# One hybrid attention/recurrence layer stack on one core: the compression of the samples' cached rows by three products of split operands in place of one full-precision product

## The reference, cut to what matters

```python
kc = compress(full(0), lp["cmp_pe"][0], lp["cmp_w1"][0], lp["cmp_w2"][0])
vc = compress(full(1), lp["cmp_pe"][1], lp["cmp_w1"][1], lp["cmp_w2"][1])
```

## Time and profile before

| | |
|---|---|
| median of 3 runs | 2860.48 us (2852.64 to 2863.11) |
| the profiled execution | 2857.92 us, its span 2855.9 us |
| mean granted TensorE clock | 0.861 of full |
| first layer: paired stage | 274 to 925 us; its compression steps lie between 274 and 557 us |
| second layer: the same | from 1694 us; its compression steps lie between 1694 and 1978 us |
| busy share | PE 81%, DVE 43%, ACT 28%, POOL 5% |

### The profile page before, as it was taken

How to read it: one execution, slowest core, us unless ns; L and a number is a source line. 1 busy time by engine, 2 the same in 40 slices (tenths; PEclk the granted TensorE clock), 3 DMA queues, 4 the chain that set the end, 5 groups by cost and what they waited for, 6 DMA issues and landing times.

```text
span 2855.9 us, 55193 instructions
## 1 busy us (share of the span) xinstructions
PE 2309.5 (81%) x22254; PEld 2086.2 (73%) x22254; DVE 1217.4 (43%) x1985; ACT 788.4 (28%) x1386; POOL 156.3 (5%) x233
## 2 busy tenths in 40 slices
PE   6986897867566889999679868878575677999995
PEld 6985676755455889999679857767453556999995
DVE  3233426254455354452332244252645454544523
ACT  3212323232223232242132132232323233322321
POOL 1000000000010000000010000000000100000000
PEclk9986898968678999999889868988686789999998
DMA  3362221212221122223123712212222211223232
GB/s 113 97 163 78 60 60 60 60 51 67 63 60 40 62 67 97 89 84 102 48 77 96 193 42 60 66 54 60 60 64 57 67 40 55 81 90 93 85 97 70
DMA packets 172775, 216.45 MB, mean 76 GB/s; under 512 B 39009, under 2 KB 138594, under 8 KB 171106
## 3 DMA queue, kind: packets, MB, share of 16 engines
q1 hardware_dynamic: 172514, 212.87, 24.9%
HBM read 204.57 MB, written 16.59 MB: 77 GB/s over the span
## 4 chain that ended last, share of the span: by engine, by line
PE 71%; DVE 16%; ACT 6%; SPq 3%; issue 3%; DMA 1%; DVEq 0%; ACTq 0%
PE ps L657 13%; PE ps L659 13%; PE ps L658 13%; PE ps L926 7%; PE ps L901 2%; PE ps L674 2%; SPq L539 2%; PE ps L819 2%; PE ps L828 1%; PE ps L894 1%; DVE arena L1631 1%; PE ps L721 1%; DVE arena L1428 1%; DVE rstd L1370 1%; DVE hf_lo L1399 1%
## 5 line engine op out<-in xcount | busy, mean ns | idle before, releaser
L657 PE MATMUL ps<-hm_hi,ring_hi 128*128 128x260 f32 x2432 | 695.5, 286 | 54.7 <-DVE hm_lo L1399 54.7
L659 PE MATMUL ps<-hm_hi,ring_lo 128*128 128x260 f32 x2432 | 692.6, 285 | 0.0
L658 PE MATMUL ps<-hm_lo,ring_hi 128*128 128x260 f32 x2432 | 690.6, 284 | 0.0
L1392 DVE TENSOR_TENSOR ring_lo<-ring,ring_hi 128x1024 fp32r<-128x1024 f32 x200 | 244.8, 1225 | 726.6 <-ACT ring_hi L1075 725.9
L657 PEld LDWEIGHTS ps<-hm_hi,ring_hi 128*128 128x128 f32 x2432 | 463.9, 191 | 57.3 <-issue 57.0
L658 PEld LDWEIGHTS ps<-hm_lo,ring_hi 128*128 128x128 f32 x2432 | 463.5, 191 | 0.3
L659 PEld LDWEIGHTS ps<-hm_hi,ring_lo 128*128 128x128 f32 x2432 | 463.4, 191 | 0.0
L1075 ACT ACTIVATE ring_hi<-ring 128x1024 fp32r<-128x1024 f32 x200 | 211.5, 1059 | 685.4 <-PE ps L659 681.6
L657 PE MATMUL ps<-hf_hi,ring_hi 128*128 128x260 f32 x704 | 203.2, 289 | 8.4 <-DVE hf_lo L1399 8.2
L659 PE MATMUL ps<-hf_hi,ring_lo 128*128 128x260 f32 x704 | 200.6, 285 | 0.0
L658 PE MATMUL ps<-hf_lo,ring_hi 128*128 128x260 f32 x704 | 200.4, 285 | 0.0
(11 more groups left out here) (362 smaller groups left out, 3943.6 us busy)
## 6 DMA issues: line engine op xcount, KB each, us to landing
ring<-in_w SPq DMA_DIRECT2D x202, 512.0 KB, 3.6
arena<-in_kv_cmp SPq DMA_DIRECT2D x96, 128.0 KB, 2.1
extra<-in_kv_cmp SPq DMA_DIRECT2D x80, 128.0 KB, 2.2
slot<-in_kv_cmp SPq DMA_DIRECT2D x80, 128.0 KB, 2.1
out_win_old<-in_win SPq DMA_DIRECT2D x16, 511.0 KB, 9.8
slot<-in_k_sel SPq DMA_DIRECT2D x96, 64.0 KB, 1.9
arena<-in_k_sel SPq DMA_DIRECT2D x96, 64.0 KB, 1.9
extra<-in_v_sel SPq DMA_DIRECT2D x96, 64.0 KB, 1.8
```

Of the source, the lines that this page charges most:

```text
L657: mmul(out, wh, hi[:, k, cols], start=(k == 0), stop=False)
L658: mmul(out, wh, lo[:, k, cols], start=False, stop=False)
L659: last = mmul(out, wl, hi[:, k, cols], start=False, stop=(ci == len(chunks) - 1 and k == k1 - 1))
L1392: v.tensor_tensor(ring_lo[:, n % RING, :], r, ring_hi[:, n % RING_HI, :], SUB).then_inc(S["w_lo"], 1)
```

## The change

Both operands of the chunk steps are split into an fp32r part and an fp32r remainder, and each of the eight fp32 matmuls becomes three fp32r matmuls (24 in a step, still 128 weight columns by 128 moving columns). The weights are split once in each layer (two steps `w1_split`: three ScalarE copies, three VectorE subtractions of 1024, 512 and 512 columns), each chunk's rows once (32 steps `chunk_split` in a layer: one ScalarE copy and one VectorE subtraction of 128x1024). The copy goes to one half of `ring_hi`, so the third slot is not used by the compression; the remainder goes over the rows in the slot. Chunk `n + 2` is split right after chunk `n` in the list, and its copy waits until chunk `n` has been read (`cmp_h`). In the planner a chunk step now weighs 2 and a split 1, where a chunk step weighed 4. The host lays out the pages so that the 16 columns of one product stand side by side. Units 0 and 1 alone are loaded ahead; unit `u` of the compression waits for the read of unit `u - 2`. The weights' copy goes over a part of `nsa` and waits for its store (`kv_stored`).

```diff
-    st = [(("qz", 0), 1)]
+    st = [(("w1_split", 0), 1), (("w1_split", 1), 1), (("qz", 0), 1), (("chunk_split", 0), 1), (("chunk_split", 1), 1)]
     for b in range(DEC):
-        st += [(("chunks", (b, q)), 4) for q in range(4)]
+        for q in range(4):
+            st += [(("chunks", (b, q)), 2)]
+            if 4 * b + q + 2 < 4 * DEC:
+                st += [(("chunk_split", 4 * b + q + 2), 1)]
+SLOT_OF = [u % 2 if u < U_WK else (u - U_WK) % USLOT for u in range(N_UNIT)]
+def before_in_slot(u):
+    mine = [w for w in range(u) if SLOT_OF[w] == SLOT_OF[u]]
+    return mine[-1] if mine else (U_WK - 1 if SLOT_OF[u] == 2 else None)
+        def units_read(eng, n):
+            if n <= U_WK:
+                eng.wait_ge(S["cmp_h"], 2 * n)
+            else:
+                eng.wait_ge(S["u_used"], n - U_WK)
-            if u >= USLOT:
-                eng.wait_ge(S["u_used"], u - USLOT + 1)
+            if before_in_slot(u) is not None:
+                units_read(eng, before_in_slot(u) + 1)
...
# TensorE, chunks
                         for k in range(STRIDE // 2):
-                            last = mmul(out, w1s[:, c, k, :], slot[:, :, c, :, k::STRIDE // 2], start=(k == 0), stop=(k == STRIDE // 2 - 1))
-                        if c:
-                            last.then_inc(S["u_used"], 1)
+                            mmul(out, w1_hi(c, k), hi[:, :, k, :], start=(k == 0), stop=False)
+                            mmul(out, w1_hi(c, k), lo[:, :, k, :], start=False, stop=False)
+                            last = mmul(out, w1s_lo[:, c, k * P:(k + 1) * P], hi[:, :, k, :], start=False, stop=(k == STRIDE // 2 - 1))
+                        last.then_inc(S["cmp_h"], 1)
...
# ScalarE
+                    if step == "w1_split":
+                        if n == 0:
+                            act.wait_ge(S["w1s_ready"], 32)
+                            act.wait_ge(S["kv_stored"], 16)
+                            A(w1h0[:], smp[:, 0:1024], ACT.Copy).then_inc(S["w1s_hi"], 1)
+                        else:
+                            for h in range(2):
+                                A(w1h1[h][:], smp[:, 1024 + 512 * h:1536 + 512 * h], ACT.Copy).then_inc(S["w1s_hi"], 1)
+                    elif step == "chunk_split":
+                        u, c = divmod(n, 2)
+                        slot = unit_landed(act, u)
+                        if u:
+                            act.wait_ge(S["cmp_h"], n - 1)
+                        A(ring_hi[:, c, :].rearrange("p (n x) -> p n x", n=PAGES // 2), chunk_view(slot, c), ACT.Copy).then_inc(S["chunk_hi"], 1)
...
# VectorE
+                    elif step == "chunk_split":
+                        u, c = divmod(n, 2)
+                        dve.wait_ge(S["chunk_hi"], n + 1)
+                        v.tensor_tensor(chunk_view(slots_lo[u % 2], c), chunk_view(slots[u % 2], c),
+                                        ring_hi[:, c, :].rearrange("p (n x) -> p n x", n=PAGES // 2), SUB).then_inc(S["chunk_lo"], 1)
...
# host
-        "kv_cmp": cache[:, :, 0:2].reshape(DEPTH * N_POOL, PAGE // 2, 2, 2, GROUPS, HD).transpose(0, 2, 5, 3, 4, 1).reshape(DEPTH * N_POOL, P, 2 * PAGE),
+        "kv_cmp": cache[:, :, 0:2].reshape(DEPTH * N_POOL, 8, STRIDE // 2, 2, 2, GROUPS, HD).transpose(0, 3, 6, 4, 2, 5, 1).reshape(DEPTH * N_POOL, P, 2 * PAGE),
```

More of the change, by code:

```diff
@@ L278, in build @@
         hm = sb("hm", [P, KB, TOK])
+        nsa_base = nc.sbuf_base
         nsa = sb("nsa", [P, NT, TOK])
@@ L302, in build @@
         arena = sb("arena", [P, ARENA])
+        extra_base = -(-nc.sbuf_base // 32) * 32
         extra = sb("extra", [P, EXTRA])
@@ L398, in build @@
         cm = at(3, HEADS)
+        where[0] += -(arena_base // 4 + where[0]) % 8
+        slot0 = where[0]
         slots = [at(2048), more(2048),
                  nc.alloc_sbuf_tensor_at("slot2", [P, 2048], F32, offset=ring_base + 4 * RING * KB * P)[:]]
+        slots_lo = [at_bytes("slot0_lo", arena_base, slot0, [P, 2048])[:], at_bytes("slot1_lo", extra_base, 0, [P, 2048])[:]]
         kcs = at(DEC, NCS)
@@ L421, in build @@
         w1s = smp[:, 0:2048].rearrange("p (c k e) -> p c k e", c=2, k=STRIDE // 2)
+        w1s_lo = at_bytes("w1s_lo", ring_base, 0, [P, 2, 1024])
+        w1h0 = at_bytes("w1h0", nsa_base, 4 * TOK, [P, 1024])
+        w1h1 = [at_bytes("w1h1", nsa_base, 7 * TOK, [P, 512]), at_bytes("w1h2", nsa_base, 9 * TOK, [P, 512])]
         w2s = smp[:, 2048:2304].rearrange("p (c e) -> p c e", c=2)
@@ L453, in build @@
                  "pc_ok pcp_ok sc_mm mx ex sc_v pt_mm pt_ev pv o_ev qpad_ok ss_mm ss_v ss_a c_free "
-                 "cmp_h cmp_act cmp_o cmp_k mixed ffn_c ffn_act ffn_h ffn_t w_hi w_lo s_hi s_lo trig_ok rs_stored phase_ok dif_ok cmp_b cmp_sum staged_a staged_v w1s_ready u_used kw_new smp_done").split()
+                 "cmp_h cmp_act cmp_o cmp_k mixed ffn_c ffn_act ffn_h ffn_t w_hi w_lo s_hi s_lo trig_ok rs_stored phase_ok dif_ok cmp_b cmp_sum staged_a staged_v w1s_ready w1s_hi w1s_lo kv_stored chunk_hi chunk_lo u_used kw_new smp_done").split()
         S = {n: ctx.enter_context(nc.semaphore(n)) for n in names}
@@ L515, in unit_landed, with w1_hi, chunk_view @@
         def unit_landed(eng, u):
-            eng.wait_ge(c_ready[u % USLOT], 16 * sum(UNIT_DMAS[u % USLOT:u + 1:USLOT]))
-            return slots[u % USLOT]
+            eng.wait_ge(c_ready[SLOT_OF[u]], 16 * sum(n for w, n in enumerate(UNIT_DMAS[:u + 1]) if SLOT_OF[w] == SLOT_OF[u]))
+            return slots[SLOT_OF[u]]
+        def units_read(eng, n):
[3 more added lines that the diff above has]
+                eng.wait_ge(S["u_used"], n - U_WK)
+        def w1_hi(c, k):
+            if c == 0:
+                return w1h0[:, k * P:(k + 1) * P]
+            return w1h1[k // 4][:, k % 4 * P:(k % 4 + 1) * P]
+        def chunk_view(a, c):
+            return a.rearrange("p (n c x) -> p n c x", n=PAGES // 2, c=2)[:, :, c, :]
         def load_unit(eng, kind, l, u):
-            slot, done = slots[u % USLOT], c_ready[u % USLOT]
-            if u >= USLOT:
-                eng.wait_ge(S["u_used"], u - USLOT + 1)
+            slot, done = slots[SLOT_OF[u]], c_ready[SLOT_OF[u]]
+            if before_in_slot(u) is not None:
+                units_read(eng, before_in_slot(u) + 1)
             if U_WK <= u < U_SK:
@@ L587, in _ @@
                 sp.dma_start(smp[:, 2048:2304], I["w2_pairs"][l]).then_inc(S["w1s_ready"], 16)
-                for u in range(USLOT):
+                for u in range(2):
                     load_unit(sp, mybir.EngineType.SP, l, u)
                 sp.wait_ge(S["nsa_ready"], 1)
-                sp.dma_start(O["kv"][l].rearrange("p (a b) -> p a b", a=6), nsa[:, 4:NT, :]).then_inc(S["stores"], 16)
+                sp.dma_start(O["kv"][l].rearrange("p (a b) -> p a b", a=6), nsa[:, 4:NT, :]).then_inc(S["kv_stored"], 16)
                 for b in range(DEC):
@@ L602, in _ @@
                         sp.dma_start(gate_r[r, h, :], gates[QD * h:QD * (h + 1), NQ, :].rearrange("b (h n) -> b h n", n=3)).then_inc(S["gs_ready"], 16)
-                for u in range(USLOT, N_UNIT):
+                for u in range(2, N_UNIT):
                     load_unit(sp, mybir.EngineType.SP, l, u)
@@ L621, in _ @@
                 sp.dma_start(O["conv_s"][l].rearrange("p (a b c) -> p a b c", a=FT, b=2), couts).then_inc(S["stores"], 16)
-                sp.wait_ge(S["stores"], 16 * (4 + DEC))
+                sp.wait_ge(S["stores"], 16 * (3 + DEC))
+                sp.wait_ge(S["kv_stored"], 16)
                 host_meet(S["arrive"], list(S.values()) + list(T.values()) + w_ready + c_ready)
@@ L918, in sample @@
                         b, (half, c) = n[0], divmod(n[1], 2)
-                        if n == (0, 0):
-                            pe.wait_ge(S["w1s_ready"], 32)
-                        elif n[1] == 0:
+                        if half == 0:
+                            pe.wait_ge(S["w1s_lo"], c + 1)
+                        if b and n[1] == 0:
                             pe.wait_ge(S["cmp_k"], b)
-                        slot = unit_landed(pe, 2 * b + half).rearrange("p (n c g t) -> p n c g t", n=PAGES // 2, c=2, g=GROUPS)
+                        u = 2 * b + half
+                        pe.wait_ge(S["chunk_lo"], 2 * u + c + 1)
+                        view = lambda a: a.rearrange("p n (k x) -> p n k x", k=STRIDE // 2)
+                        hi = view(ring_hi[:, c, :].rearrange("p (n x) -> p n x", n=PAGES // 2))
+                        lo = view(chunk_view(slots_lo[u % 2], c))
                         out = W4[:, c, :, CH * half:CH * (half + 1)].rearrange("p g (n t) -> p n g t", n=PAGES // 2)
                         for k in range(STRIDE // 2):
-                            last = mmul(out, w1s[:, c, k, :], slot[:, :, c, :, k::STRIDE // 2], start=(k == 0), stop=(k == STRIDE // 2 - 1))
-                        if c:
-                            last.then_inc(S["u_used"], 1)
+                            mmul(out, w1_hi(c, k), hi[:, :, k, :], start=(k == 0), stop=False)
```

(22 more changed lines are left out.)

4 lines of the change are left out of this document (2 added, 2 removed).

## The result

The change makes the kernel slower: 2976.9 us as the median of 4 runs against 2861.8, ratio 1.0407 (95% interval 1.038 to 1.0435), some 116 us. The prediction said 2838, and 2790 to 2895 for the range.

The account below looks back on a forecast made before the run. PE was taken to bound most of the compression, DVE the starts of recurrence blocks. Products -46, splits +20 and +9, selected-unit wait -5 gave -22 us on 2857.9: 2836, or 2838 as a median; range 2790 to 2895.

Parts of the forecast that it names:

- split products near the clock of before, with list, slots and weights' split: Chunk steps and list: 46 us gained by the split products, 5 by a shorter wait for selected units.
- the clock: PE's granted clock: the sum had no term for a change of it, only 9 us off for steps already at half.
- the splits: ACT and DVE split work: 20 us lost in DVE-bound stretches, weights included, and 9 us elsewhere at 0.2 a split.
- A split product's cost: PE's chunk steps: the weight load holds each product to 0.112 us at full clock, 0.215 at half.
- Rival 1: Chunk steps: 128-column products fall back to fp32's rate, 0.218 us each; 2954 us and more; 14%.
- rival 4: Chunk steps: the load does not hold the product, which costs 0.059 us; 2770 us; 8%.
- The share at half clock: Of 25 counted chunk steps a layer, four started at half clock, each costing 1.1 us more; 9 us off the gain.
- Rival 2: The splits stand in the chain, delaying evacuations by 1 us each, with load waits showing; say 2880 us; 17%.
- The DVE-bound start: Stretches where recurrence blocks begin: splits add 6 us in the first, 4 in the second; 20 lost over both layers.
- The loads: Compression's unit loads with two slots: ACT waits 2 to 4 us about once a sample; counted as nothing, bounds 0 and 42.
- The rest of the paired stage: Selected blocks' steps lie further apart, so the wait for a selected unit halves; 5 us gained over two layers.
- The rows at 387.36: Trace of an old chunk step at half clock: 4.04 us, hardly longer, so that form was not bound by TensorE's clock.

Follow-up runs that it names:

- e7: The changed kernel with rows split only once in a layer and each product's 128 columns streamed twice; 2816.2 us, ratio 0.9844.
- e2: The changed kernel with rows split only once in a layer, later copies, all subtractions and waits on them left out; 2870.8 us, ratio 1.0079.
- e4: The changed kernel with all its splits, each of the 24 products streaming its 128 columns twice; 2912.6 us, ratio 1.0206.
- e9: The changed kernel with doubled columns, split waits kept, copy and subtraction cut to 8 columns after the first unit, low rows unread; 2866.6 us, ratio 1.0046.
- e10: The changed kernel with doubled columns, split waits and ACT's full copies kept, only DVE's subtractions cut to 8 columns, low rows unread; 2875.1 us, ratio 1.0075.
- e6: The kernel before with the new page layout, unsplit fp32 products, and the changed kernel's list, two slots and loads; 2748.0 us, ratio 0.9617.
- e5: The kernel before with the new page layout, unsplit fp32 products and the changed kernel's list, split steps empty; 2753.8 us, ratio 0.9639.

## Why the prediction was wrong

The terms of the sum, with what the runs give for each. The measured ones are steps from one run to the next, so they add up to 116 by construction; each is uncertain by 9 to 12 us.

| term, us, minus is a gain | forecast | measured | from |
|---|---|---|---|
| split products near the clock of before, with list, slots and weights' split | -51 | -45 (partly luck, see e7) | e7 to before |
| the clock | 0 | +67 | e2 to e7 (+57 by changed to e4) |
| the splits (forecast with the weights', measured without) | +29 | +94 | changed to e2 (+103 by e4 to e7) |

- **A split product's cost: right.** I took 0.112 us between 0.106 and 0.119; it is 0.112 at full clock and 0.213 at half (0.215 forecast). The weight load holds it, as read from the earlier trace rows: twice the columns cost 0.009 us (e4). Rival 1 (0.218 at full clock, four passes) and rival 4 (0.059) are both refuted. The Trainium skill ("TensorE: Matmul & The Clock Gate", section "Back-to-back issue gap") gives 81 ns for a pair of load and product at 128 columns. The trace does not agree for this form: it has 112 ns.
- **The share at half clock: the first step that failed.** I wrote that a step at half clock costs 1.1 us more and counted "four of these", those of the 9 of before that start in the PE-bound stretches; the sum has no term for a change of the clock. 40 steps of 64 started there. The old form took 0.233 us a record at either clock, so the clock of before had cost it little; the new form takes nearly twice as long at half clock, 2.4 us more a step. For 31 more such steps that is, by estimate, 75 us. That is a price I had worked out and then multiplied with a count that the change itself moves. The runs give 57 to 67, and not in the chunk steps alone: from e2 to e7 they are 12 of the 27 us that the first layer's two blocks gain, and other work of PE the rest.
- **The splits: the second step that failed.** I counted 0.2 us for each split in the PE-bound stretches, from DVE's idle 8 and 10 us, and wrote as the upper bound 105 us "if each stood in the chain". The start's 20 and that bound make 125; measured are 94 to 103. The idle time of DVE is time in which it waits for PE, and the split's copy waits for the same PE (`cmp_h`): the split starts when the idle time ends, in front of all that the chunk's end sets free. With the columns doubled, 58 of the 103 us are such waits, 37 the length of DVE's subtraction (e9, e10). Rival 2 named this mechanism but priced it too low: with the clock held up by doubled columns (e4) the kernel takes 2913 us, where the rival said 2880.
- **The DVE-bound start.** Forecast 20 us for both layers. In the first of them PE waits 11.6 us at L922: DVE stands at its second subtraction for ACT's copy, which is behind ACT's work for the recurrence. The waits of a split across two engines were not in the term, only its busy time. DVE's first long reciprocal (the block's `RECIPROCAL` of 128x512) starts at 306.9 us, in e2 at 294.0: 13 us for this one start, where the forecast took 6.

The timeline of DVE there, in the changed kernel:

```profile
287.13 1.23 DVE L1717 TENSOR_TENSOR slot_lo<-arena,ring_hi 128x1024 fp32r<-128x1024 f32 x1 [1.71 <-ACT ring_hi L1281]
294.41 1.23 DVE L1717 TENSOR_TENSOR slot_lo<-arena,ring_hi 128x1024 fp32r<-128x1024 f32 x1 [6.06 <-ACT ring_hi L1281]
...
306.88 3.35 DVE L1483 RECIPROCAL arena<-arena 128x512 f32<-128x512 f32 x1
```

And in e2:

```profile
293.96 3.35 DVE L1481 RECIPROCAL arena<-arena 128x512 f32<-128x512 f32 x1
```

- **The loads: nothing speaks against the forecast.** ACT waits 20.1 us for landings in both layers, in 6 pieces, where I had expected one of 2 to 4 us in each of 16 samples. e6 shows that two slots cost nothing without the splits; with the splits no run takes their cost alone:

```profile
  PE ps L968: 151.0, 32
  DMA arena<-in_kv_cmp: 20.1, 6
```

The first of these lines, ACT's 151.0 us of waiting for PE before 32 of its 64 copies, is the one that tells of the order.
- **The rest of the paired stage: right in sign, too small in size.** It is 12 us a layer shorter, where I had forecast 5 in both: later steps lie further apart. PE's wait for a selected unit, 5.7 us in the first layer before, is gone. e5 shows the last two blocks' gain with no split at all, 9 us a layer.
- **Three readings.** The second layer's chunk steps span 282 us, as the first's do, not 288. What follows a chunk step starts without a wait in 56 of 64 cases, not 54. The fp32 records of 24 columns start 0.112 us apart in the trace; 0.106 came from spreading their first, shorter distance over all. So the cost of a load, and of a split product, stood in the trace before. None of the three changes the forecast.

The two failures are not independent, though no run here takes the one fully from the other: the splits' work alone takes the steps at half clock from 26 (e2) to 40, the doubled columns take them from 26 to 14 (e7) and from 40 to 18 (e4). With the columns doubled the splits' waits alone leave 11 (e9), so there they do not bring the clock down. At half clock the load-bound products are nearly twice as long. The rows at 387.36 showed a chunk that did not care; that comfort went with the form of its read.

## What to carry to other kernels

Before splitting an fp32 product, look at how its moving operand is read: a step of 8 floats cost a factor of 2.1 here, and the layout alone made the kernel 3% faster, 3.8% with the list and slots of the change, where the split form with 128 columns had to pay three weight loads for two. When a product is bound by its weight load, work its cost out at both clocks and ask how many will run at each after the change, for the count of before belongs to the form of before. An engine that idles because it waits for PE has no room for work that waits for the same PE; what stands behind that work in its queue is late by the whole of it.

## What the runs showed of the hardware that I had not expected

- fp32r products of 128 by 128 with 128 columns start 0.112 us apart at 2.4 GHz and 0.213 at 1.2 GHz; with 256 columns 0.121 and 0.213. The second 128 columns are nearly free.
- fp32 records with contiguous columns take the same 0.112 and 0.213, with a step of 8 floats 0.233 and 0.237, nearly the same at both clocks.
- With the same loads, splits and waits, the granted clock of the first block was 0.64 with 128 columns for each load and 0.79 with 256; without the splits' work 0.76 and 0.85.
